# Weight sums of the Strassen products: from a chain of DMAs per chunk to batches in a DRAM scratch

## What is computed

```python
h = rmsnorm(x, p['norm_mix_pre'])
mix, ... = token_mixers(h, ...)          # hgrn: S_new = exp(G_last) * S + (k * exp(G_last - G)).T @ v
x = x + rmsnorm(mix, p['norm_mix_post'])
h = rmsnorm(x, p['norm_ffn_pre'])
u = h @ p['w_ffn_up']                    # 1024 x 2*2816
a, v = u[..., :D_FF], u[..., D_FF:]
c = p['ffn_conv_b'] + sum(ext[:, j:j + T] * w[j] for j in range(CONV_W))
out = (jax.nn.silu(c) * v) @ p['w_ffn_down']
x = x + rmsnorm(out, p['norm_ffn_post'])
```

## Time and profile before

| | |
|---|---|
| median of three runs | 1934.43 us (1931.81 to 1935.34) |
| profiled execution | 1932.28 us, of which the span is 1930.5 us |
| PE busy | 1820.8 us, 94% of the span |
| DVE, ACT, POOL busy | 1267.4, 951.0, 229.5 us |
| mean granted TensorE clock | 0.979 |
| DMA | 204.03 MB, 106 GB/s over the span |

### The profile page before, as it was taken

How to read it: one execution, slowest core, us unless ns; L and a number is a source line. 1 busy time by engine, 2 the same in 40 slices (tenths; PEclk the granted TensorE clock), 3 DMA queues, 4 the chain that set the end, 5 groups by cost and what they waited for, 6 DMA issues and landing times.

```text
span 1930.5 us, 31256 instructions
## 1 busy us (share of the span) xinstructions
PE 1820.8 (94%) x11636; PEld 1668.9 (86%) x11636; DVE 1267.4 (66%) x1973; ACT 951.0 (49%) x1593; POOL 229.5 (12%) x257
## 2 busy tenths in 40 slices
PE   8999999999899999898799999999998999999985
PEld 7999975698899999898799999657988999999984
DVE  5777875526765665677767778653377665756776
ACT  5444546436653443535654444653466343535355
POOL 0000034100112121111000000340001111111100
PEclk9999999999999999999999999999999999999997
DMA  4312131411565665565131122323125565556621
GB/s 178 91 57 68 62 95 52 134 54 40 130 159 142 153 142 141 138 156 140 44 106 46 57 68 72 88 74 96 60 76 145 142 151 143 141 149 166 140 71 60
DMA packets 98902, 204.03 MB, mean 106 GB/s; under 512 B 16864, under 2 KB 35680, under 8 KB 98728
## 3 DMA queue, kind: packets, MB, share of 16 engines
q1 hardware_dynamic: 63952, 144.39, 23.5%
q0 software_dynamic: 21888, 39.86, 12.6%
q10 hardware_dynamic: 12912, 17.78, 2.8%
HBM read 170.98 MB, written 8.65 MB: 93 GB/s over the span
## 4 chain that ended last, share of the span: by engine, by line
PE 56%; DVE 17%; DMA 13%; ACT 9%; issue 3%; DVEq 0%; POOL 0%; ACTq 0%; SPq 0%; POOLq 0%
PE G L795 34%; PE WA L795 11%; PE WB L795 8%; DVE wlo L2158 5%; DMA t<-in_wstream 4%; DMA wraw<-in_wstream 2%; ACT whi L1480 2%; DMA t<-wraw 2%; DVE tmp L2158 2%; DMA wff<-in_wstream 2%; DVE cc L2158 1%; DMA wraw<-t 1%; DMA wff<-t 1%; PE G L799 1%; DVE ax L2158 1%
## 5 line engine op out<-in xcount | busy, mean ns | idle before, releaser
L795 PE MATMUL G<-Hh,wlo 128*128 128x328 f32 x1384 | 452.4, 327 | 11.8 <-DVE Hl L2158 8.0
L795 PE MATMUL G<-Hh,whi 128*128 128x328 f32 x1384 | 436.0, 315 | 0.0
L795 PE MATMUL G<-Hl,whi 128*128 128x328 f32 x1384 | 434.6, 314 | 0.0
L795 PEld LDWEIGHTS G<-Hh,wlo 128*128 128x128 f32 x1384 | 263.2, 190 | 23.3 <-DVE Hl L2158 12.1
L795 PEld LDWEIGHTS G<-Hh,whi 128*128 128x128 f32 x1384 | 263.4, 190 | 2.4 <-issue 0.6
L795 PEld LDWEIGHTS G<-Hl,whi 128*128 128x128 f32 x1384 | 263.1, 190 | 0.0
L1480 ACT ACTIVATE whi<-wraw 128x1024 fp32r<-128x1024 f32 (+2 forms) x171 | 155.6, 910 | 187.0 <-PE G L795 114.7
L2158 DVE TENSOR_TENSOR wlo<-wraw,whi 128x1024 fp32r<-128x1024 f32 (+2 forms) x171 | 177.6, 1038 | 54.4 <-ACT whi L1480 41.8
L795 PE MATMUL G<-gh,wlo 128*128 128x328 f32 x424 | 134.3, 317 | 10.1 <-DVE tmp L2158 9.3
L795 PE MATMUL G<-Sh,wlo 128*128 128x328 f32 x304 | 100.9, 332 | 34.2 <-ACT R L1480 34.2
L795 PE MATMUL G<-gh,whi 128*128 128x328 f32 x424 | 132.9, 313 | 0.0
(11 more groups left out here) (327 smaller groups left out, 4142.9 us busy)
## 6 DMA issues: line engine op xcount, KB each, us to landing
wraw<-in_wstream SPq DMA_DIRECT2D x108, 512.0 KB, 3.5
wff<-in_wstream SPq DMA_DIRECT2D x40, 512.0 KB, 4.6
t<-in_wstream SPq DMA_DIRECT2D x76, 256.0 KB, 4.4
t<-in_wstream POOLq DMA_DIRECT2D x38, 256.0 KB, 6.5
ckT<-in_ckT SPq DMA_DIRECT2D x12, 512.0 KB, 3.4
wff<-in_wstream POOLq DMA_DIRECT2D x20, 256.0 KB, 4.1
t<-wff POOLq DMA_DIRECT2D x20, 256.0 KB, 3.9
wff<-t POOLq DMA_DIRECT2D x20, 256.0 KB, 3.5
```

What stands on the lines that cost most here:

```text
L795: return pe.matmul(out, lhsT, rhs, start=start, stop=stop, skip_group_check=True)
```

## The change

A DRAM tensor `wsum` takes the four sums of each of the 19 chunks of a layer as one row block [T2 T3 | T1 T4]. POOL makes them in five batches of 4, 4, 3, 4 and 4 chunks by DRAM to DRAM DMAs: copies of u, v.right and v.left, then accumulating DMAs for T1 and T3, T2, and T4, each behind a wait for the batch's earlier ones. Three batches stand at the head of a layer's work on POOL, ahead of the first head's decay, and two right behind that decay. The first starts when four tiles are done.

In the channel mixer SP now loads four pieces for a chunk, u, [T2 T3], [T1 T4] and v.right, into five slots in turn; `t2` and `t3` are gone. (T1, T4) is split as a pair in place of (T4, B22), and DVE's g_low(2) stands ahead of the sums of activations at the first group's end.

```diff
-RAW, SPL = 2, 3
+RAW, SPL, SLOTS = 2, 3, 5
...
-LATE = {B11: 1, B21: 0, T2: 1, T3: 0, T1: 0, T4: 1, B22: 0}
-PAIRS = (B11, T2, T4)
+LATE = {B11: 1, B21: 0, T2: 1, T3: 0, T1: 1, T4: 0, B22: 0}
+PAIRS = (B11, T2, T1)
+CHUNK_PIECES = 4
...
+BATCHES = [(NPL, 7), (7, FH), (FH, 14), (14, 18), (18, KF)]
...
+    wsum = nc.dram_tensor("wsum", [DEPTH, NS, P, 2 * W_PIECE], F32, kind="Internal").ap()
...
-        wff = sb(ff, "wff", [P, 2, W_PIECE])
-        t23 = sb(ff, "t23", [P, 3, W_HALF])
+        wff = sb(ff, "wff", [P, SLOTS - RAW, W_PIECE])
...
         def raw_slot(p):
-            return p % 2 if p < P_UP + 2 * NPL else p % 4
+            return p % RAW if p < P_UP + 2 * NPL else (p - P_UP) % SLOTS
...
+        def summing(l, b):
+            n = l * len(BATCHES) + b
+            return f"sums{n % 3}", 112 * (n // 3)
...
                 for c, p0 in P_CHUNK.items():
                     if p == p0 + 1:
-                        sum_parts(l, c)
+                        name, n = summing(l, next(b for b, (c0, c1) in enumerate(BATCHES) if c0 <= c < c1))
+                        sp.wait_ge(S(name), n + 112)
...
+            def start_sums(l, b):
+                (u, v, t), (name, n) = stored_parts(l, b), summing(l, b)
+                if n:
+                    pool.wait_ge(S(name), n)
+                pool.dma_start(t[:, :, W_PIECE:2 * W_PIECE], u).then_inc(S(name), 16)
+                pool.dma_start(t[:, :, to_t2], v[:, :, right]).then_inc(S(name), 16)
+                pool.dma_start(t[:, :, to_t3], v[:, :, left]).then_inc(S(name), 16)
+
+            def sum_t1_t3(l, b):
+                (u, v, t), (name, n) = stored_parts(l, b), summing(l, b)
+                pool.wait_ge(S(name), n + 48)
+                pool.dma_start(t[:, :, to_t1], v[:, :, left], accum_op=ALU.add).then_inc(S(name), 16)
+                pool.dma_start(t[:, :, to_t3], v[:, :, right], accum_op=ALU.add).then_inc(S(name), 16)
+
+            def sum_t2(l, b):
+                t, (name, n) = stored_parts(l, b)[2], summing(l, b)
+                pool.wait_ge(S(name), n + 80)
+                pool.dma_start(t[:, :, to_t2], t[:, :, to_t1], accum_op=ALU.add).then_inc(S(name), 16)
+
+            def sum_t4(l, b):
+                t, (name, n) = stored_parts(l, b)[2], summing(l, b)
+                pool.wait_ge(S(name), n + 96)
+                pool.dma_start(t[:, :, to_t4], t[:, :, to_t2], accum_op=ALU.add).then_inc(S(name), 16)
+
+            def weight_sums(l, b0, b1):
+                for b in range(b0, b1):
+                    start_sums(l, b)
+                for b in range(b0, b1):
+                    sum_t1_t3(l, b)
+                for b in range(b0, b1):
+                    sum_t2(l, b)
+                for b in range(b0, b1):
+                    sum_t4(l, b)
+
+            pool.wait_ge(S("tile"), 4)
             for l in range(DEPTH):
+                weight_sums(l, 0, 3)
                 for h in range(HG):
...
                     decay_state(l, h)
+                    if h == 0:
+                        weight_sums(l, 3, len(BATCHES))
...
                 split_out(l, range(HG))
-                sum_t1(l, NPL)
-                sum_t2(l, NPL)
-                for c in range(NPL, KF):
-                    sum_t3(l, c)
-                    sum_t4(l, c)
...
                         lows(l, u0 - 1)
+                        g_low(last_c)
...
-                    g_low(last_c)
+                    if q:
+                        g_low(last_c)
```

More of the change, by code:

```diff
@@ L257, in raw_slot @@
         def raw_slot(p):
[L258 removed]
+            return p % RAW if p < P_UP + 2 * NPL else (p - P_UP) % SLOTS
         def raw_of(p):
[L261 removed]
+            s = raw_slot(p)
+            return wraw[:, s, :] if s < RAW else wff[:, s - RAW, :]
         def last_unit(p):
             for c, p0 in P_CHUNK.items():
[L266 to L267 removed]
+                if p0 <= p < p0 + CHUNK_PIECES:
+                    return U_PROD[c] + (B21, T3, T4, B22)[p - p0]
             return next((U_PASS[q] + p - p0 for q, p0 in P_PASS.items() if p0 <= p < p0 + GROUPS[q][1] - GROUPS[q][0]), p)
@@ L356, in raw_unit @@
             c, i = product_of(u)
[L357 to L360, removed]
+            return raw_of(P_CHUNK[c] + i // 2)[:, W_HALF * (i % 2):W_HALF * (i % 2) + W_HALF]
         def raw_ready(g):
@@ L367, in raw_ready @@
             c, i = product_of(u)
[L368 to L377, removed]
+            return loaded[l * PIECES + P_CHUNK[c] + i // 2]
+        def summing(l, b):
+            n = l * len(BATCHES) + b
+            return f"sums{n % 3}", 112 * (n // 3)
         def act_took(l, c, i):
@@ L650, in _ @@
                     sp.wait_ge(S("out"), 32 * (l + 1))
-                for s, lo, hi, at in parts_of(p):
-                    sp.dma_start(raw_of(p)[:, at:at + hi - lo], a["wstream"][l, s][:, lo:hi]).then_inc(S(loaded[g][0]), 16)
                 for c, p0 in P_CHUNK.items():
                     if p == p0 + 1:
-                        sum_parts(l, c)
+                        name, n = summing(l, next(b for b, (c0, c1) in enumerate(BATCHES) if c0 <= c < c1))
+                        sp.wait_ge(S(name), n + 112)
+                for s, lo, hi, at in parts_of(p):
+                    of = a["wstream"][l, s] if s is not None else \
+                        wsum[l, next(c for c, p0 in P_CHUNK.items() if p0 <= p < p0 + CHUNK_PIECES) - NPL]
+                    sp.dma_start(raw_of(p)[:, at:at + hi - lo], of[:, lo:hi]).then_inc(S(loaded[g][0]), 16)
                 if g % PIECES == 6:
@@ L742, in sum_t2 @@
[L742 to L754, removed]
@@ L756, in sum_t4, with stored_parts @@
-            def sum_t4(l, c):
-                j, w = chunk_no(l, c), raw_of(P_CHUNK[c])
-                pool.wait_ge(S("w_split"), unit_of(j, B21) + 1)
-                sum_wait(l, c, T2)
-                pool.dma_start(w[:, W_HALF:W_PIECE], t2[:, j % 2, :], accum_op=ALU.add).then_inc(S("T"), 16)
+            def stored_parts(l, b):
+                c0, c1 = BATCHES[b]
+                s, n = S_UP[c0 // FH] + 2 * (c0 % FH), c1 - c0
+                return a["wstream"][l, s:s + 2 * n - 1:2], a["wstream"][l, s + 1:s + 2 * n:2], wsum[l, c0 - NPL:c1 - NPL]
@@ new lines, in _ @@
+            left, right = slice(0, W_HALF), slice(W_HALF, W_PIECE)
+            to_t2, to_t3, to_t1, to_t4 = (slice(W_HALF * i, W_HALF * i + W_HALF) for i in range(4))
+            def start_sums(l, b):
[5 more added lines that the diff above has]
+                pool.dma_start(t[:, :, to_t3], v[:, :, left]).then_inc(S(name), 16)
```

39 lines of the change are left out of this document (7 added, 32 removed).

## The result

The changed kernel takes 2135.1 us (median of four runs, 2134.4 to 2137.2) against 1934.6 us (four runs): a ratio of 1.104, with a 95% interval of 1.102 to 1.106. The forecast was 2040 in a range of 1965 to 2165. The direction and the mechanism were right. The size was 95 us short.

The account below looks back on a forecast made before the run. PE was taken as bound by accumulating DMAs through ACT in the mixer and the decay chain at layer start. Stalls 138 + clock 5 + contention 3 - mixer gain 40 = +106 us on 1932.3, plus 2.1: 2040, range 1965 to 2165.

Parts of the forecast that it names:

- What bounds the kernel: Mixer: accumulating DMAs through ACT, 34.2 us of PE waits; layer start: decay, new state, Z, PE, under 1 us slack.
- Part 1: Channel mixer: PE's waits on R go and the clock recovers; gain 40 us, ends 15 to 44.
- Parts 2 to 4: Stalls at layer 0's first two decays and layer 1's decay: 46, 44 and 27 us; 138 taken in all.
- the queue's price: Sums' DMAs: q0's 1.60 us per 256 KB accumulated, copies 0.82; 8.1 us a chunk, T4 another 1.6.
- the factor of 1.17: Sums' DMAs: a DRAM source lands later than SBUF, 4.1 against 3.5 us; stalls 158 us in place of 118.
- rival D: Sums' DMAs: DRAM on both sides doubles the price, 354 us of stalls; 2256 us; chance 10%.
- Part 4: Layer 1: first three batches load the engines in attention, 3 us; two batches behind the first decay stall 27 us.
- the forecast's own mechanism: Stalls at the decays, at 0.9 to 1.4 of the queue's price: 1985 to 2120 us; chance 60%.
- A: Sums end before the first decay is due and nothing waits, at 472 GB/s: 1893 us, about 1897 by the skill; chance 6%.
- B: Sums' accumulates cost no more than loads, stalls at their low end of 46 us: 1944 us; chance 8%.
- C: Mixer: ACT's waits become waits on DVE, or `wsum` loads come late; only 15 us won: 2065 us; chance 14%.
- The signs: Profile after: first decay at 155 to 170 us, DVE waiting 46 to 62 on POOL, DMA share near 1 from 51.

Follow-up runs that it names:

- the run with gaps cut to size: Changed kernel with T1 and T3 chunk by chunk, batches 0 to 2 divided around the decays, 3 and 4 behind chunk 6's first split: 1901.2 us, 0.9833.

## Why the prediction was right, and where it was 95 us short

**What bounds the kernel: right.** The chain decay, new state, Z, PE had under 1 us of slack, and PE lost what the decay lost. The run that took 86.5 us from the three gaps, and the last one, which has none, both show it. (The first matmuls behind the gaps are `WB<-sq,ones`, a little ahead of Z in PE's order; the waiting is on the same state.)

**Part 1, the mixer's gain: 40 forecast, 36 measured.** Waits on R fell to 0.7 us, and the kernel without sums gives the whole: 1897.2. What was late next cost little: one wait of PE, on ACT's Y at the mixer's start in layer 1, grew by 1 us. The sums' loads stayed hidden, and the move of g_low(2) cost nothing that the traces show. (By the prediction's own rows, 0.16 against 0.27 us, the lower clock loses 41% and not 43, which makes 16 us of its 17 and changes nothing else.)

**Parts 2 to 4, the stalls: right in kind, too small.** At the queue's price the working gave 46, 44 and 27 us, 117 in all; I then took 138. Measured were 85.0, 62.6 and 57.9. The step that failed is the one that gave every accumulate the price of q0's 128-row DMAs, and with it took engine time for elapsed time: it spread each DMA over all 16 engines. It did not ask whether the new ones had the same shape, and T1 and T3 of a batch kept only three or four engines busy each. With T1 and T3 issued chunk by chunk the gaps are 47.4, 38.2 and 33.5 us, 119.1 in all: the queue's price without any factor was within 2 us for the sum (the parts are off by +1, -6 and +7 us and partly cancel), and q0's share, 18.4% of 2029.6 us in that run, is 373 us against the 369 of the prediction. So the factor of 1.17 for a source in DRAM was not needed, nor rival D's doubling. The 86.5 us between are the skip in the source of T1 and T3, and nothing in the trace of before has a DMA like that. Even then q0 holds the engines for 17.9% of 2133.0 us, 382 us, in the kernel after: busy time of the engines gave no sign of it, only elapsed time did. The prediction's price in engine time was right, then, and what it had wrong is how many engines share it.

**Part 4, 3 us for contention: the step that was missing.** I priced the layer-1 batches by the engines' free share. What they hit was one small transfer with much behind it: `cout<-in_cst` landed after 30.4 us in place of 4, at the head of the mixer, where ACT, DVE and PE all follow from it. That was 18 us, and 22 of the time. In attention it was 4.2 against the 3 taken.

**Luck.** The range of 1965 to 2165 held the result, but the range of the forecast's own mechanism, 1985 to 2120, did not. Its upper end was there for rival D, a dearer engine price with DRAM on both sides, which the runs refute. No part of the range and no rival was for engines left idle by the shape of a DMA, so that 2135 fell inside was in part luck. The mechanism, POOL's waits ahead of the decays, was not.

**The rivals.** A named 472 GB/s as the point from which the sums would hide; the copies came to 350 with the loads beside them, and the engines over a stretch of accumulates by chunk to 159 (1190 to 1220 us of that run, share 0.96; the prediction's q0 rate was 164), so it was not reached. The Trainium skill, DMA: Bandwidth & Descriptors, "Anatomy of one DMA — SWDGE (gpsimd) path", gives 436 GB/s for a DMA from POOL once its fixed time has passed. The trace doesn't reach it: the 350 GB/s of the copies are the highest of the stretches shown here. But A's time of 1893 and 1897 is what the run with gaps cut to size nearly reaches (1901), by place and not by rate. B, accumulates as cheap as loads, fell: they cost the 1.60 us of the queue's price even chunk by chunk. C fell: the gain came. SP never waited for sums in the kernel after; it did (122.9 us) as soon as they were moved late.

**The signs.** First decay forecast at 155 to 170, DVE's waits at 46 to 62: measured 193.84 and up to 85.3. DMA share near 1 from 51 us on: so for 59 to 85 (1.02), and not behind it (0.61). That sign was the first to tell that the missing time was not load.

## What to carry to other kernels

- A wait on an engine that works in order is paid by everything behind it. Moving large asynchronous work off a critical engine means to find, in the timeline, idle gaps that hold each step with its landing (28 us for a batch's copies, 20 for T1 and T3, 12 for T2 here), and to issue only the next step in each. The same sums then cost 4 us in place of 238; of the difference about 105 us are the form of T1 and T3 with the late small transfer, and the rest is place.
- Price a DMA by a row of the same shape. If source rows have a skip in them, issue the parts one by one, and look at the DMA share while one such DMA runs alone: it tells how many engines have work.
- Before flooding the queues, look for small transfers on the critical chain in the same stretch, and let them land first.

## What the hardware showed that I had not expected

- A DMA of POOL whose source skips a piece between chunks kept as many DMA engines busy as it had chunks: shares of 0.28 and 0.21 with four and three chunks, beside 1.12 without the skip, and 92 GB/s at a share of 0.61 over 40 us of such accumulates. The same bytes and the same number of DMAs from rows at one distance took 103 us less of the kernel's time (2135.1 to 2031.7), the mixer's 18 among them.
- POOL stood for 26.3 us at its eighth large copy (85.48), waiting for nothing that the profile names ("issue"), while the first seven had gone out at 1.1 us each. In layer 1's batches it was the eighth again that stood, for 33.5 us. So with seven copies of 1 to 2 MB in flight POOL could not issue another; where exactly the limit lies, no run here shows.
- A transfer of 176 KB took 30.4 us beside the sums in place of 4.0. Nothing else lost as much: a `cpe` load of 64 KB took 6.2 to 7.7 us in place of 3.4, and pieces of 512 KB landed in 7.9 at the height of the copies, in place of 3.5 in the kernel without sums. What sets the first apart, no run here shows.
